# Two ScalarE steps on the forget gates placed behind the split of the next weight unit, in a four-layer block on one Trainium2 core

## What is computed

```
def hgrn2_layer(x, norm_w, w_in, lb, out_norm_w, w_out):
    h = rmsnorm(x, norm_w)
    proj = h @ w_in                      # q, fz, i, gate: 2048 columns each, 16 heads of 128
    ...
    log_f = jnp.logaddexp(jnp.log(lb), jnp.log1p(-lb) + jax.nn.log_sigmoid(fz))
    k = (1.0 - lb) * jax.nn.sigmoid(-fz)
    o = hgrn2_chunkwise(q, k, i, log_f)
    o = head_rmsnorm(o.transpose(0, 2, 1, 3), out_norm_w.reshape(HG_HEADS, HG_VDIM))
    o = o.reshape(B, T, D_MODEL) * jax.nn.silu(gate.astype(jnp.float32))
    return x + (o.astype(x.dtype) @ w_out)

# hgrn2_chunkwise:  S_t = diag(exp g_t) S_{t-1} + k_t v_t^T ;  o_t = S_t^T q_t ;  g = log_f
```

## Time and profile before

| | before |
|---|---|
| median of 3 runs | 1857.76 us (1857.69 to 1859.28) |
| the profiled execution's own time | 1856.62 us |
| its span, first to last instruction | 1854.8 us |
| TensorE busy | 1828.5 us (99%), 8827 matmuls |
| VectorE busy | 1259.7 us (68%) |
| ScalarE busy | 956.4 us (52%) |
| mean granted TensorE clock | 0.997 of full speed |

### The profile page before, as it was taken

One profiled execution on the slowest core, in us unless ns is written; L12 is line 12 of the kernel. 1 busy time (PEld: TensorE's weight loads), 2 busy tenths in 40 slices (PEclk: granted clock), 3 DMA queues, 4 the chain that ended last, 5 costly groups with the idle time before them and its releaser, 6 DMA issues.

```text
span 1854.8 us, 24335 instructions
## 1 busy us (share of the span) xinstructions
PE 1828.5 (99%) x8827; PEld 1533.8 (83%) x8827; DVE 1259.7 (68%) x1692; ACT 956.4 (52%) x1323; POOL 38.2 (2%) x114
## 2 busy tenths in 40 slices
PE   8999999999999999999999999999999999999999
PEld 6888888887888888887787887878888888888887
DVE  5566666588557755768787868777766555577764
ACT  4555554455455545536554545545435444565542
POOL 2000000000000004000000000000000000000000
PEclk9999999999999999999999999999999999999999
DMA  8555454667789887665554554544556666545453
GB/s 276 170 170 149 137 170 143 212 179 167 183 153 211 176 182 165 202 236 155 167 171 145 161 170 147 171 146 159 175 148 204 183 191 191 160 150 173 155 170 114
DMA packets 169867, 319.25 MB, mean 172 GB/s; under 512 B 16264, under 2 KB 20512, under 8 KB 169008
## 3 DMA queue, kind: packets, MB, share of 16 engines
q1 hardware_dynamic: 168656, 313.69, 58.7%
q10 hardware_dynamic: 576, 4.19, 0.5%
q0 software_dynamic: 544, 0.13, 0.1%
HBM read 315.88 MB, written 2.10 MB: 171 GB/s over the span
## 4 chain that ended last, share of the span: by engine, by line
PE 48%; DVE 2%; issue 1%; ACT 0%; DVEq 0%; ACTq 0%
PE acc L298 14%; PE acc L300 14%; PE acc L299 14%; PE ps L2656 2%; PE ps L540 1%; DVE arena L2043 1%; PE ps L393 0%; PE ps L2645 0%; PE ps L2742 0%; DVE wlo L267 0%; PE ps L2637 0%; PE ps L573 0%; ACT whi L259 0%; DVE arena L2030 0%; DVE arena L2031 0%
## 5 line engine op out<-in xcount | busy, mean ns | idle before, releaser
L267 DVE TENSOR_TENSOR wlo<-wraw,whi 128x1024 fp32r<-128x1024 f32 (+1 forms) x595 | 714.9, 1216 | 377.5 <-ACT whi L259 374.5
L259 ACT ACTIVATE whi<-wraw 128x1024 fp32r<-128x1024 f32 (+1 forms) x595 | 613.1, 1046 | 333.1 <-PE acc L300 330.6
L298 PE MATMUL acc<-whi,ta_hi 128*128 128x512 f32 x1664 | 662.4, 398 | 12.3 <-DVE wlo L267 12.3
L300 PE MATMUL acc<-whi,ta_lo 128*128 128x512 f32 x1664 | 650.3, 391 | 0.0
L299 PE MATMUL acc<-wlo,ta_hi 128*128 128x512 f32 x1664 | 649.8, 390 | 0.0
L298 PEld LDWEIGHTS acc<-whi,ta_hi 128*128 128x128 f32 x1664 | 313.8, 189 | 78.7 <-DVE wlo L267 14.0
L300 PEld LDWEIGHTS acc<-whi,ta_lo 128*128 128x128 f32 x1664 | 313.5, 188 | 66.9
L299 PEld LDWEIGHTS acc<-wlo,ta_hi 128*128 128x128 f32 x1664 | 314.1, 189 | 62.1
L298 PE MATMUL acc<-whi,tb_hi 128*128 128x512 f32 (+1 forms) x704 | 276.7, 393 | 0.0
L300 PE MATMUL acc<-whi,tb_lo 128*128 128x512 f32 (+1 forms) x704 | 271.5, 386 | 0.0
L299 PE MATMUL acc<-wlo,tb_hi 128*128 128x512 f32 (+1 forms) x704 | 271.1, 385 | 0.0
(11 more groups left out here) (314 smaller groups left out, 1354.3 us busy)
## 6 DMA issues: line engine op xcount, KB each, us to landing
wraw<-in_ml_w_in SPq DMA_DIRECT2D x129, 512.0 KB, 5.8
wraw<-in_a_w_in SPq DMA_DIRECT2D x128, 512.0 KB, 3.9
wraw<-in_kv_w SPq DMA_DIRECT2D x64, 512.0 KB, 3.8
wraw<-in_b_w_in SPq DMA_DIRECT2D x64, 512.0 KB, 4.3
wraw<-in_mla_w_in SPq DMA_DIRECT2D x49, 512.0 KB, 4.5
wraw<-in_mla_w_out SPq DMA_DIRECT2D x32, 512.0 KB, 3.8
wraw<-in_ml_w_out SPq DMA_DIRECT2D x32, 512.0 KB, 4.5
wraw<-in_a_w_out SPq DMA_DIRECT2D x32, 512.0 KB, 3.7
```

Of the source, the lines that this page charges most:

```text
L259: nc.scalar.activation(unit_of(whi, n, SPLIT, w), unit_of(wraw, n, RAW, w), ACT.Copy).then_inc(w_high, 1)
L267: nc.vector.tensor_tensor(unit_of(wlo, n, SPLIT, w), unit_of(wraw, n, RAW, w), unit_of(whi, n, SPLIT, w).bitcast(F32), ALU.subtract).then_ ...
L298: nc.tensor.matmul(o, xh, wh, start=first, stop=False)
L300: m = nc.tensor.matmul(o, xl, wh, start=False, stop=end)
```

## The change

ScalarE's function `turned()` keeps the copy of the queries. The wait for `nf`, Exp and Ln become a function `forget()`, which is called one unit later, at u = 20, so behind `high` of unit 20. Nothing is added or left out, and no other engine's program changes. The names' line numbers move: from the Exp on by 2, from the call of `turned()` on by 4.

```
@@ -1320,6 +1320,8 @@
                 def turned():
                     act.wait_ge(l2["tq"], 1 + g)
                     nc.scalar.activation(flat(qT2), ps2(0), ACT.Copy).then_inc(l2["qT"], 1)
+
+                def forget():
                     act.wait_ge(l2["nf"], 1 + g)
                     nc.scalar.activation(dT[:, 0, :], dT[:, 0, :], ACT.Exp).then_inc(l2["lf"], 1)
                     act.wait_ge(l2["lf"], 1 + 2 * g)
@@ -1374,6 +1376,8 @@
 
                 if u == L2_AT["turn"] + LAG:
                     turned()
+                if u == L2_AT["turn"] + LAG + 1:
+                    forget()
                 if u == L2_AT["diag"] + LAG - 1:
                     keys()
                 if u == L2_AT["diag"] + LAG:
```

## The result

| | before | after |
|---|---|---|
| median of the runs | 1857.72 us (1857.59 to 1859.28, 4 runs) | 1844.12 us (1843.08 to 1844.82, 4 runs) |
| ratio, 95% interval | | 0.9925 [0.9912, 0.9937] |
| the profiled execution's own time | 1856.62 us | 1843.94 us |
| its span | 1854.8 us | 1842.1 us |
| mean granted clock in the profile | 0.997 | 1.000 |

The kernel is 13.6 us faster, 0.7%. The forecast was 1844.0.

A forecast was written before the change was run, and what follows sets the result against it. TensorE's own work was taken to bound the kernel, plus four third-layer waits and the half clock behind three. Waits 8.3 and clock 4.6 make 12.9 us off 1856.62, 1843.7, put at 1844.0; range 1842 to 1849.8.

The forecast's parts named there:

- What bounds the kernel: TensorE's own work, plus third-layer waits at unit 21's first product, 2.33 us in group 0, 2.36 in groups 1 to 3.
- The high half costs nothing: On ScalarE, unit 20's high half, about 1.05 us, fits into 2.36 us of idle time; Exp and Ln start as before.
- 2.08 us per group: VectorE's decay step starts 2.08 us earlier, shortening TensorE's wait at unit 21 as much: 4 x 2.08 = 8.3 us.
- The clock: TensorE's three falls to half clock behind the waits of groups 1 to 3 all go: 4.56 us.
- The page against the rows: By the page's second rule, TensorE's remaining 0.44 us waits could still bring clock falls, group 0 included: 1849.8 us.
- What TensorE runs into: TensorE comes closer behind VectorE at later steps; group 0's level 0 shows 2.2 us in hand, so costed at nothing.
- The waits shrank and the clock did not fall all the same: Rival at TensorE's unit 21: waits shrink but the clock still falls, gain 8.3 us (1848.3) or 6.8 (1849.8); chance 0.10.
- something changed: Answers the rival that nothing changes, VectorE's run being late for a second reason: 1856.6 to 1857.8 us; chance 0.04.
- The slower rival: TensorE waits anew at level 0 for VectorE's operands, 4.9 us late, and the clock falls: some 1861 us; chance 0.02.

The follow-up runs named there:

- forget gates first: The changed kernel with the forget gates transposed ahead of the queries: 1841.21 us, ratio 0.9911.
- one unit further: The changed kernel with Exp and Ln one unit later still, behind the high halves of units 20 and 21: 1847.94 us, ratio 0.9946.
- the kernel with group 0 alone: The kernel before with Exp and Ln moved behind the high half of unit 20 in group 0 only: 1854.11 us, ratio 0.9978.
- second series: The changed kernel measured again with nothing altered: 1844.61 us, ratio 0.9924.
- both kernels with the later scans: VectorE's decay step with its scans put behind the low half of unit 21, in the kernel before (1848.83 us) and in the changed kernel (1843.68 us).
- the move by three units: The changed kernel with Exp and Ln behind the high halves of units 20, 21 and 22: 1868.36 us, ratio 1.0062.

## Why the prediction was right, point by point

*What bounds the kernel.* Right. The four waits at unit 21 were all of the third layer's loss; when the last rest of them goes (forget gates first), nothing is left there.

*The high half costs nothing.* Right: Exp starts 3.39 us behind the start of the copy in both kernels. The text named the idle time as the cover and the order of TensorE's program as the reason why the copy can start. The runs show that the second matters as much: one unit further the idle time would have been enough (2 x 0.97 us in 2.36), and the second high half was not ready to go.

*2.08 us per group.* Measured 2.07 on VectorE, and the waits went from 2.33 and 2.36 to 0.33 and 0.28 or 0.29. Both conditions of the decay step, VectorE's own run and Ln's end, were worked out; they fall together here (1219.03 and 1219.06), so either alone would have given nearly the same number.

*The clock.* In the profiles right: 4.56 us were taken from the three stretches behind the waits, and with 8.3 they make the 12.9 measured over the layer. That all three would go was a choice made from short waits in one trace; the runs bear it out, but with 2.36 us followed by the full clock in the kernel with group 0 alone nothing shows why. In the medians the term was mis-sized. I had priced three falls, those of the profiled execution. Of the 33 runs of the kernel before that stand beside the experiments, 6 have a mean clock of 0.997, 21 of 0.996 and 6 of 0.995; nearly all of the first take 1856.0 to 1856.3 us, the second 1857.4 to 1858.2, the third 1859.2 to 1859.7. The steps are the 1.5 to 1.7 us of one fall, and the profiled execution with its three falls is of the first kind. So the usual execution has four, worth some 6.1 us. That number is read off sums; only profiles show the places. In the changed kernel a part of the executions has one left: the profile of its second series has a clock of 0.87 at 372 to 376 us and 0.70 in the next 4 us, the layer change, and 1.00 in the third layer. Four falls gone and now and then one left make 8.3 + 6.1 - (0 to 1.6), that is 12.8 to 14.4, and 13.6 were measured. That the forecast lies within 0.2 us of the median is therefore partly luck: a fourth fall that was not priced before, and a fall that is left in some executions afterwards, offset each other in part.

*The page against the rows.* The Trainium skill (TensorE: Matmul & The Clock Gate, "A second HAM failure mode") describes a kernel whose clock swings because TensorE idles very shortly, and often, between groups of products. The prediction carried this over to single waits and got 1849.8 us from it. That did not come about: behind eight waits of 0.28 to 0.33 us in the two profiles of the changed kernel the clock stays at 1.00. But these waits stand some 102 us apart, so no run here shows what frequent ones would do.

*What TensorE runs into.* Right in its result, loose in its number. I took 2.2 us of reserve from level 0. The smallest reserve of group 2 in the changed kernel is at levels 5 and 6, 1.3 and 1.2 us, and both kernels with the later scans ran into it.

*The rivals.* The waits shrank and the clock did not fall all the same; something changed; no new wait appeared. The slower rival needed VectorE 4.9 us late and would have had a nearer place than level 0. A slower kernel did come by another way: with the move by three units, Exp late by the waits of the high halves.

## What to carry to other kernels

On an engine whose queue is in order, look for a wait that has an instruction behind it which needs nothing of what is waited for, and follow that instruction to the engine that sets the time. Put it in front if its own conditions are met by then; count each further one by what it waits for, not by how long it runs. Price the half clock behind TensorE's waits from several executions, and before moving work later on the engine that feeds TensorE, look up the smallest reserve in the whole group and not only the first.

## What the runs showed of the hardware

How often TensorE's clock falls behind a wait goes with the wait's length, and not with it alone. Counted over the twelve profiles of this study (before, changed twice, nine others):

| idle time ahead of the product | places | clock fell behind it |
|---|---|---|
| 4.17 to 4.27 us | 4 | 4 |
| 2.33 to 2.36 us | 8 | 5 |
| 1.60 and 0.48 us, layer changes | 24 | 3 |
| 1.45 to 1.55 us | 8 | 0 |
| 1.23 to 1.27 us | 4 | 0 |
| 0.28 to 0.33 us | 12 | 0 |

Waits of 0.15 to 0.73 us elsewhere, most of them ahead of transposes at the layer changes, near 449 us and in the kernels with the later scans, are left out; no slow products follow them. The waits for the first loads, in the first 18 us, are left out too.

A fall costs 1.4 to 1.6 us behind waits of 2.36 us and at the layer changes, about two thirds of such a wait again, and 1.3 to 2.8 us behind those of 4.17 to 4.27 us. I had expected it to come with the wait's length; that a wait of 2.36 us in the same program brings it in one group and not in the next I had not. What decides between them stays open: no run held the wait and varied something else.
